# A one-layer decoder step on one core: order of work at the front, in the prompt attention and in the tail

## The reference, cut to what matters

```
h = x + W_out[ rms(NSA(n)) ; rms(ShortConv(n)) ],  n = rmsnorm(x)
h = h + PEER(rmsnorm(h))                    # 8 heads x 16 experts of one neuron a token
y = h + sigmoid(rmsnorm(h) W_g) * (p W_p)   # W_g 2048 x 2048, W_p 256 x 2048
```

## Time and profile before

| what | us |
| --- | --- |
| median of 3 runs (lowest, highest) | 2547.03 (2544.01, 2556.1) |
| the profiled execution, and its span | 2548.46, span 2546.6 |
| PE busy / DVE / ACT / POOL | 1701.0 / 1151.5 / 334.1 / 915.6 |
| chain that ended last: DMA / PE / DVE / issue | 46% / 39% / 6% / 3% |

### The profile page before, as it was taken

The page is one execution under the profiler, slowest core; times in us unless marked ns, Lnnn a source line. Parts: engine busy times, 40 slices in busy tenths (PEclk is TensorE's granted clock), DMA queues, the critical chain, the costliest instruction groups (busy, mean ns, idle before and its releaser), DMA issues.

```text
span 2546.6 us, 21559 instructions
## 1 busy us (share of the span) xinstructions
PE 1701.0 (67%) x8372; PEld 921.9 (36%) x8372; DVE 1151.5 (45%) x2141; ACT 334.1 (13%) x731; POOL 915.6 (36%) x644
## 2 busy tenths in 40 slices
PE   7999998998987668788787333323233333577677
PEld 3445675696775347433475000000000000122224
DVE  2010213124455763544533666566665665544342
ACT  1000232010001322200100101101011002001002
POOL 0000000013223453422433565656666555555430
PEclk9998996998998776599698666666666565787788
DMA  8953373779999998999998999999999999999996
GB/s 316 351 180 114 114 291 112 269 245 412 388 377 379 362 382 311 394 390 385 415 410 338 420 418 421 421 421 421 422 421 422 421 421 417 399 416 416 416 418 224
DMA packets 215845, 908.75 MB, mean 357 GB/s; under 512 B 17351, under 2 KB 40880, under 8 KB 131809
## 3 DMA queue, kind: packets, MB, share of 16 engines
...
...
## 4 chain that ended last, share of the span: by engine, by line
DMA 46%; PE 39%; DVE 6%; issue 3%; POOL 3%; ACT 3%; SPq 0%; DVEq 0%; PEldq 0%; ACTq 0%; POOLq 0%
DMA arena<-in_peer_v,arena 19%; DMA arena<-in_peer_u,arena 15%; PE bank L1725 9%; DMA arena<-in_w_in 5%; PE bank L2175 4%; PE bank L2160 4%; DVE arena L1521 3%; DMA arena<-in_w_out 3%; PE bank L1799 2%; DMA arena<-in_peer_wq 2%; PE bank L1936 2%; PE bank L1912 2%; PE bank L2109 2%; DMA arena<-in_state_win 2%; PE bank L2284 2%
## 5 line engine op out<-in xcount | busy, mean ns | idle before, releaser
L1521 DVE CUSTOM_DVE_ANT_0 arena<-arena 128x2048 f32<-128x2048 f32 x320 | 730.8, 2292 | 581.2 <-DMA arena<-in_peer_u,arena 577.9
L2160 PE MATMUL bank<-arena 128*32 128x512 f32 x2560 | 463.4, 828 | 670.8 <-DVE arena L1530 523.7
L675 POOL DMA_INDIRECT arena<-in_peer_u,arena x320 | 566.2, 1769 | 862.1 <-DVEq L1500 577.1
L680 POOL DMA_INDIRECT arena<-in_peer_v,arena x320 | 349.1, 1091 | 691.0 <-PE bank L2160 663.7
L2160 PEld LDWEIGHTS bank<-arena 128*32 128x32 f32 x2560 | 68.8, 127 | 1004.5 <-DVE arena L1530 508.4
L1725 PE MATMUL bank<-arena 128*128 128x512 f32 (+2 forms) x544 | 217.0, 559 | 5.3 <-PE bank L1725 2.6
L2175 PE MATMUL bank<-arena 128*128 128x192 f32 x1024 | 188.2, 346 | 25.6 <-DMA arena<-in_w_in 24.1
L2175 PEld LDWEIGHTS bank<-arena 128*128 128x128 f32 x1024 | 179.7, 203 | 46.9 <-DMA arena<-in_w_in 31.3
L1725 PEld LDWEIGHTS bank<-arena 128*128 128x128 f32 (+1 forms) x544 | 101.4, 208 | 117.2 <-issue 116.8
L987 ACT ACTIVATE arena<-arena 128x4 f32<-128x4 f32 x80 | 16.8, 211 | 864.1 <-DVE arena L1521 863.9
L2284 PE MATMUL bank<-arena 128*128 128x512 f32 x256 | 124.8, 647 | 0.0
...
## 6 DMA issues: line engine op xcount, KB each, us to landing
arena<-in_w_in SPq DMA_DIRECT2D x22, 2048.0 KB, 9.2
...
arena<-in_w_out SPq DMA_DIRECT2D x8, 2048.0 KB, 9.8
arena<-in_peer_wq SPq DMA_DIRECT2D x8, 2048.0 KB, 8.3
...
arena<-in_ple_gate SPq DMA_DIRECT2D x6, 2048.0 KB, 12.2
```

Source lines behind the costliest of these rows:

```text
L675: pool.indirect_dma_start(u_row[j], None, I["peer_u"][0], bass.IndirectOffsetOnAxis(idx[:, i, c + j:c + j + 1], 0)).then_inc(u_in[j], 16)
L680: pool.indirect_dma_start(v_row[j], None, I["peer_v"][0], bass.IndirectOffsetOnAxis(idx[:, i, c + j:c + j + 1], 0)).then_inc(v_in[j], 16)
L1521: dve.tensor_tensor_reduce(out=u_row[j], in0=u_row[j], in1=rep_of(i), scale=1.0, scalar=0.0, op0=ALU.mult, op1=ALU.add, accum_out=a4[:, pa ...
L2160: ins = pe.matmul(bank[i % 2][32 * q:32 * q + 32, :], diag[:, k % 2, j, :], v_row[j][:, 512 * q:512 * q + 512], start=(s == 0 and j == 0), ...
```

## The change

1. **Front loads.** The ten small loads are issued by ACT; SP starts with `cst` and tile 0, and loads weight block 1 ahead of the other two token tiles.
2. **Front transposes.** Tile 0's 16 chunks go four to a bank into banks 4 to 7 with no wait between them; DVE alone copies each bank in one operation of 128 x 512. The squares of tile 0 no longer wait for the other tiles.
3. **Compression.** DVE copies the even groups out of bank 6, ACT the odd ones out of bank 7.
4. **Attention.** The order for a head becomes `turn_probs(u)`, `scores(u+2)`, `head_sums(u-1)`, `values(u)`.
5. **Gate.** Quarters 28 and 29 run ahead of the value rows of step i = 14. `sample_ple(0)` and `(1)` run inside quarter 24, `(2)` and `(3)` ahead of the value rows of step 15, all into banks of their own (2 to 5). Their loads and the last prompt sigmoid and `prompt_y(3)` move forward with them.
6. **Tail.** The last sum is copied, added, transposed and multiplied in four quarters of 512 columns. Block 2's weights are issued without the embedding loads ahead of them.

```diff
...
-        for i, name in enumerate(("norm1", "norm2", "norm3", "out_gain")):
-            sp.dma_start(gain_rows[KC * i:KC * i + KC, :], I[name][0].rearrange("(k p) -> k p", p=128)).then_inc(gains_in, 16)
...
-        sp.dma_start(tab[0:NBUCKET, :], I["rel_bias"]).then_inc(first_in, 16)
         sp.dma_start(cst, I["cst"]).then_inc(cst_in, 16)
         sp.dma_start(h[:, 0, :], xp[0]).then_inc(x0_in, 16)
...
         fill_z(0)
+        fill_z(1)
         sp.dma_start(h[:, 1, :], xp[1]).then_inc(x_in, 16)
         sp.dma_start(h[0:64, 2, :], xs).then_inc(x_in, 16)
         sp.dma_start(h[64:128, 2, :], xs).then_inc(x_in, 16)
-        fill_z(1)
         sp.dma_start(pages[0:1, :], I["page_table"].rearrange("(o b) n -> o (b n)", o=1)).then_inc(small_in, 16)
...
+        ple_load(4)
+        ple_load(5)
         y_out(2)
...
         for i in range(1, 4):
...
                      w_view["gate"][:, 8 * half:8 * half + 8, 512 * LAST_COLS[i]:512 * LAST_COLS[i] + 512])
-            if i == 1:
-                ple_load(4)
-                ple_load(5)
-        y_out(3)
+            if i == 2:
+                y_out(3)
...
     def _(act):
+        for i, name in enumerate(("norm1", "norm2", "norm3", "out_gain")):
+            act.dma_start(gain_rows[KC * i:KC * i + KC, :], I[name][0].rearrange("(k p) -> k p", p=128)).then_inc(gains_in, 16)
...
+        act.dma_start(tab[0:NBUCKET, :], I["rel_bias"]).then_inc(first_in, 16)
         act.sem_inc(mm_ev, 2)
...
         act.wait_ge(turn_ev, 1)
-        odd_transposes(KC, lambda e, c: e.activation(xT[:, c, 0:128], bank[7][:, 0:128], ACT.Copy, scale=gT[:, 0, c:c + 1]))
         root(stats[:, 0:3], stats[:, 3:6])
...
-            for c in range(NB + 2):
+            for c in range(1, NB + 2, 2):
                 act.wait_ge(t_mm, tcount[0] + c + 1)
-                src = bank[6 + c % 2]
+                src = bank[7]
...
-                ins.then_inc(t_ev[c % 2], 1)
+                ins.then_inc(t_ev[1], 1)
             tcount[0] += NB + 2
...
             for q in range(4):
                 ins = act.activation(acc[r:r + 32, 512 * q:512 * q + 512], bank[i % 2][32 * q:32 * q + 32, :], ACT.Copy)
-            ins.then_inc(acc_ev, 1)
+                if i == SUBS - 1 or q == 3:
+                    ins.then_inc(acc_ev, 1)
...
-            if i in (6, 9, 12):
+            if i in (6, 9, 12, 15):
                 gate_sigmoid((i - 6) // 3)
             gelu(k)
...
-        gate_sigmoid(3)
-        odd_transposes(KC, lambda e, c: e.activation(hT_s[:, c, :], bank[7][:, 0:64], ACT.Copy, scale=gT[:, 2, c:c + 1]))
         root(stats[:, 146:147], stats[:, 149:150])
...
-        even_transposes(KC, lambda e, c: e.tensor_scalar(xT[:, c, 0:128], bank[6][:, 0:128], gT[:, 0, c:c + 1], None, ALU.mult))
+        for c in range(0, KC, 4):
+            dve.wait_ge(turn_mm, c // 4 + 2)
+            dve.tensor_tensor(xT[:, c:c + 4, 0:128], bank[4 + c // 4][:, :].rearrange("p (c t) -> p c t", c=4),
+                              rep(gT[:, 0, c:c + 1], [1, 4], [0, 128]), ALU.mult).then_inc(turn_ev, 1)
         dve.wait_ge(x0_in, 16)
-        dve.wait_ge(x_in, 48)
         for t in range(3):
+            if t == 1:
+                dve.wait_ge(x_in, 48)
             ins = squares(h[:, t, :], junk[:, t, :], stats[:, t:t + 1])
         step(ins)
...
+        def raw_out(kind):
+            even_transposes(NB + 2, lambda e, c: e.tensor_copy(
+                raw[kind][:, :, 2 * c:2 * c + 2, :].rearrange("p m s c -> p s c m"),
+                bank[6][:, :].rearrange("p (s c m) -> p s c m", s=2, m=STRIDE)))
+        dve.wait_ge(xn_ready, 1)
+        raw_out(0)
         dve.wait_ge(small_in, 16 * 2)
         dve.wait_ge(mm_ev, 2 + 12)
...
-        tcount[0] += 2 * (NB + 2)
-        evens[0] += NB + 2
-        odds[0] += NB + 2
+        dve.wait_ge(xn_out, 32)
+        raw_out(1)
         even_transposes(12, heads_out)
...
         extra = {2: lambda: (gate_rms(), hT_out(0)), 3: lambda: hT_out(1),
-                 6: lambda: prompt_y(0), 9: lambda: prompt_y(1), 12: lambda: prompt_y(2)}
+                 6: lambda: prompt_y(0), 9: lambda: prompt_y(1), 12: lambda: prompt_y(2), 15: lambda: prompt_y(3)}
...
-        prompt_y(3)
-        add_peer(SUBS - 1)
-        even_transposes(KC, lambda e, c: e.tensor_scalar(hT_s[:, c, :], bank[6][:, 0:64], gT[:, 2, c:c + 1], None, ALU.mult))
...
+        def last_turned(q):
+            dve.wait_ge(hT_mm, 2 + q + 1)
+            dve.tensor_tensor(hT_s[:, 4 * q:4 * q + 4, :], bank[6 + q % 2][:, 0:256].rearrange("p (c t) -> p c t", c=4),
+                              rep(gT[:, 2, 4 * q:4 * q + 1], [1, 4], [0, 64]), ALU.mult).then_inc(hT_ev, 1)
+        for q in range(4):
+            dve.wait_ge(acc_ev, SUBS + q)
+            v = h[32:64, 2, 512 * q:512 * q + 512]
+            dve.tensor_tensor(v, acc[32:64, 512 * q:512 * q + 512], v, ALU.add).then_inc(h_seen, 1)
+            if q:
+                last_turned(q - 1)
+        last_turned(3)
+        dve.wait_ge(h_seen, SUBS + 3)
         step(squares(h[0:64, 2, :], acc[0:64, :], stats[0:64, 146:147]))
         inv_rms(stats[:, 146:147], stats[:, 146:147], stats[:, 149:150], stats[:, 160:161], D)
         dve.sem_inc(h_ready, 1)
...
             s = sig[0:64, blk % 2, :]
-            step(dve.tensor_tensor(s, s, bank[4 + blk % 2][0:64, :], ALU.mult))
-            dve.sem_inc(ple_mm, 1)
+            step(dve.tensor_tensor(s, s, bank[PLE_BANK[blk]][0:64, :], ALU.mult))
...
         pe.transpose(bank[1][:, 0:97], gain_rows[0:97, :], ident[0:97, 0:97]).then_inc(turn_mm, 1)
         pe.wait_ge(x0_in, 16)
-        transposes(KC, tok_tiles(x_tile, (0,)))
-        pe.wait_ge(t_ev[0], 8)
-        pe.wait_ge(t_ev[1], 8)
+        for c in range(KC):
+            ins = pe.transpose(bank[4 + c // 4][:, 128 * (c % 4):128 * (c % 4) + 128], x_tile(0, c), ident)
+            if c % 4 == 3:
+                ins.then_inc(turn_mm, 1)
+        pe.wait_ge(turn_ev, 5)
...
         for u in range(NH):
+            turn_probs(u)
             if u < NH - 2:
                 scores(u + 2)
-            turn_probs(u)
-            values(u)
             if u:
                 head_sums(u - 1)
+            values(u)
         def out_part(n, part):
...
+        def sample_ple(i):
+            slot = LAST_COLS[i] % 2
+            if i >= 2:
+                pe.wait_ge(ple_in[slot], 16 * 3)
+            for c in range(2):
+                ins = pe.matmul(bank[PLE_BANK[i]][0:64, :], pleT[:, c, 256:TOK], ple_w[slot][:, c, :],
+                                start=(c == 0), stop=(c == 1))
+            ins.then_inc(ple_used, 1)
+        def prompt_gate(q):
+            blk, part = divmod(q, 8)
+            if part == 0:
+                if blk == 0:
+                    pe.wait_ge(hT_ev, 4)
+                else:
+                    pe.wait_ge(y_ready, blk)
+                pe.wait_ge(ple_in[blk % 2], 16 * (blk // 2 + 1))
+                for t in range(2):
+                    for c in range(2):
+                        ins = pe.matmul(bank[6 + t][:, :], pleT[:, c, 128 * t:128 * t + 128], ple_w[blk % 2][:, c, :],
+                                        start=(c == 0), stop=(c == 1))
+                ins.then_inc(ple_used, 1)
+                if blk == 3:
+                    sample_ple(0)
+                    sample_ple(1)
+            pe.wait_ge(gw_in[gate_slot(q)], 16 * (q // GW + 1 if q < 29 else 1))
+            for t in range(2):
+                for k in range(2):
+                    ins = pe.matmul(bank[4 + t][:, :], hT[:, 2 * part + k, 128 * t:128 * t + 128], gate_w[gate_slot(q)][:, k, :],
+                                    start=(part == 0 and k == 0), stop=(part == 7 and k == 1))
+            ins.then_inc(gw_used, 1)
+            if part == 7:
+                pe.wait_ge(gw_used, q + 1)
+                pe.sem_inc(gate_mm, 1)
...
         for i in range(2 * SSTEP):
+            if i == 2 * SSTEP - 1:
+                pe.wait_ge(sig_ready, 4)
+                sample_ple(2)
+                sample_ple(3)
+            if i == 2 * SSTEP - 2:
+                prompt_gate(28)
+                prompt_gate(29)
             weighted_rows(LAST + i)
...
             for q in gate_quarters(i):
...
+                if i < 14 or q >= 30:
+                    prompt_gate(q)
...
+        def last_turn(q):
+            pe.wait_ge(h_seen, SUBS + q)
+            if q >= 2:
+                pe.wait_ge(hT_ev, 4 + q - 1)
+            for c in range(4 * q, 4 * q + 4):
+                ins = pe.transpose(bank[6 + q % 2][:, 64 * (c % 4):64 * (c % 4) + 64], h[0:64, 2, 128 * c:128 * c + 128],
+                                   ident[0:64, 0:64])
+            ins.then_inc(hT_mm, 1)
+        def first_gate(q):
+            pe.wait_ge(hT_ev, 4 + q + 1)
+            for c in range(4 * q, 4 * q + 4):
+                ins = sample_gate(0, c, gate_w[gate_slot(24 + c // 2)][:, c % 2, :], c == 0, c == KC - 1)
+            return ins
         pe.wait_ge(y_ready, 4)
-        sample_ple(0)
```

(18 more changed lines are left out.)

62 lines of the change are left out of this document (17 added, 45 removed).

## The result

The changed kernel took a median of 2525.5 us over four runs (2523.4 to 2527.4), the kernel before, beside it, 2551.3 (2544.0 to 2556.1, four runs): a ratio of 0.9905, 95% interval 0.9887 to 0.9922. The forecast was 2516.0 with a range of 2507 to 2528. So it is faster by about 1%, with 1 outside the interval, and inside the forecast's range; 24 to 26 us of the forecast 31 arrived. The page of the changed kernel: its span is 2524.0 us against 2546.6, a difference of 22.6.

What follows compares the result with a forecast made beforehand. Transfers were taken to bound the middle, PE's chain the front and the tail. The terms 7.8 + 2.6 + 1.2 + 0.7 + 18.7 = 31.0 us, off the median 2547.03, gave 2516.0 us, range 2507 to 2528.

Steps and rivals of the forecast that it cites:

- (A): Front: transfers start no earlier or tiles 1 and 2 come too late; front term -3.9, time 2519.9; chance 0.12.
- (B): Tail: bound by its weights or PE's clock; tail -13.5, time 2521.2; chance 0.14.
- Front: Front loads and tile 0's transposes: first product at 12.8 in place of 20.63, 7.8 us earlier.
- The cover of tiles 1 and 2: Front: token tiles land at 36.8, ACT may start on the first product at about 43, just as PE finishes the second.
- Compression: Compression's transposes: 1.8 us for two groups with copies shared by DVE and ACT, gaining 2.6 first and 1.2 the second time.
- Attention: Attention heads: the new order removes PE's 0.62 us wait for ACT's copy, entered as a gain of 0.7 us.
- Rival (C): Attention: the denser order brings PE's clock back to 2.4 GHz, -4 to -6 us more, time 2511; chance 0.09.
- Gate: Last expert steps: quarters 28 and 29 fill PE's 4.78 us wait, transfers stay queued, last value row unmoved: 0.
- the prediction's own sign of being wrong: Middle: wrong if the distance from the start of the gathers to the last value row changes by more than 3 us.
- Tail: Behind the last value row: first product 2.6 us later, four blocks without embedding products between; gain 18.7 us.
- Rival (E): Middle: PE's gain at the front is absorbed by transfers that are not moved, leaving the tail, 2528.3; chance 0.06.
- Rival (D): Middle: the gathers lose rate and it ends slower than before, 32 us lost at 3%; chance 0.04.

Runs made afterwards that it cites:

- e9_best: Changed kernel without the reload of the embedding columns, and with the gains' turn between the two halves of tile 0; 2517.9 us, ratio 0.9876.
- e7_split: Changed kernel with half of tile 0 turned before the wait for the gains, and the first half-product waiting for two copies only; 2523.2 us, ratio 0.9881.
- e8_delay: Changed kernel without the embedding reloads, and with the last gate columns' first two weight loads held until the last four v rows start; 2522.6 us, ratio 0.9888.
- e3_front: Kernel before with the front's edits alone (loads and tile 0's transposes); 2543.7 us, ratio 0.9970.
- e2_rest: Changed kernel with the tail as before, so front, compression and attention edits only; 2534.5 us, ratio 0.9940.

## Why the prediction was right, and where it was off

Right in direction and range, but outside 2511 to 2520, where the prediction had put most of its chances. The measured time lies where (A) and (B) were expected, but (A) came only in part, and (B) not in the first trace. The forecast gain was 31.0 us; the runs give 24 to 26, and the terms as the traces show them add up to that. Each term by its own step:

- **Front, forecast 7.8, measured 6.7** at 217 us, behind the first outputs (6.6 to 7.9 over the seven traces with this front), and 6.0 to 6.8 at the first product. The new start of the first product was put at 12.8, on the weights. It came at 13.8 to 14.7 in the seven traces with this front. The weights let PE start at 13.2 to 13.5 (`e9_best`, `e7_split`), up to 0.7 later than the old landing time moved by 3.9. Above that stood what the step passed over with "ACT has no work then, and PE needs them only when tile 0 lands": the gains are there at 9.0 to 9.9, after tile 0 at 7.7, and the four copies cost 0.69 each, within the bound of 0.8. The cover of tiles 1 and 2 held, as narrowly as forecast: ACT starts on the first product at 44.7, not 43, the second block ends there, and the third starts 6.2 us earlier than before (56.07 against 62.30). In `e7_split`, where PE is there sooner, this cover runs out. Rival (A) was half right; the loads started in time, and the small ones were late.
- **Compression, forecast 2.6 and 1.2, measured 2.7 and 0.3.** The second number failed in "the same sum gives -1.2". The sum is 2.25 less 1.78 for two groups, but the prediction itself had 7.25 / 8 = 0.91 for a group the second time, so 1.81 less 1.78: next to nothing. The term was mis-sized by using the first row for both places.
- **Attention, forecast 0.7, measured 0.8** (0.6 to 1.0 in eight of the nine traces that have the edit, 3.4 in `e8_delay`): period 4.50, clock 0.50, and 1.30 of wait for heads 6 and 7 (1.25 forecast). The size is luck. The pieces that the prediction lists are a gain of six times 0.5 and losses of 1.3 and twice 1.2; they add up to a loss of 0.7, and it was entered as a gain. In the two traces heads 0 to 4 gain 0.4 to 0.6 each and head 5 loses 0.2; heads 6 and 7 lose 0.65 each and not 1.2, for a head took 3.85 there before and takes 4.50 now; and of the 1.3 for `scores(2)` nothing shows, since PE still waits 3.1 us for DVE ahead of head 0. Half a microsecond goes back behind the heads, where the first 16 output products take 9.27 us instead of 8.78. Rival (C), the return of the clock, did not come. The Trainium skill (TensorE: Matmul & The Clock Gate, "What's actually happening") lets activity release the throttle; with PE busy 4.56 of 5.00 us by the profile the grant stayed at 0.50, so this trace doesn't agree for this stretch.
- **Gate, forecast 0, measured a loss of 2.2 to 2.8** (the last v row against the 201st u gather, in four traces). The failing step is "Transfers stay queued meanwhile (...), so nothing runs dry: 0". Nothing ran dry, but the change also moves the two embedding loads, 1 MB, ahead of the last gathers, and these bytes were priced nowhere. The traffic row that says the queue stays full also gives their price: 1 MB at 416 GB/s is 2.5 us. The distance from the start of the gathers to the last value row was named as the test, with 3 us as the limit. It moved by 6.1 us in the first trace and 6.7 in the second, so the prediction's own sign of being wrong came; of the 6.1, 3.8 belong to the spread of the middle and 2.3 to the stretch behind the 201st gather.
- **Tail, forecast 18.7, measured 18.4** from the last value row to the last product (53.1 to 34.7) in the first trace. Counted from the last v row it is 18.0 there and 17.2 as the mean of four traces. Its steps hold one by one in the first: 2.7 for 2.6 to the first product, 9.7 for block 0 where 8.7 + 1.4 was given, 7.13 and 0.30 for the others, weights just in time. Three other traces with this tail gave 36.5 to 38.0 from the last v row to the last product, against 36.2; in the longest the granted clock up to the second block was lower (0.70 for 0.77).
- **Rival (E), the middle absorbs the front**: had a chance of 0.06, looked true in the first pair of traces (10.7 became 6.8), and is refuted: `e3_front` keeps 6.9 at the median and `e2_rest` 16.1. Rival (D) did not come; the gathers' rate is 421 in both.
- **The base.** 2547.03 was the median of three runs; the runs beside the changed kernel gave 2551.3. The absolute forecast was 9.5 us too low: 5.2 of missing gain (31.0 against 25.8) and 4.3 of base. From the old base the same gain would have given 2521.2.

Sum by the traces: front 6.7, compression 3.0, attention 0.8, tail 17.2 (mean of four traces, from the last v row: 54.2 to 37.0), less 2.5 for the reloads: 25.2, against 26.3 by the medians of all runs.
